# Attention pairs turned through two banks at once, a reciprocal of two columns, and packed score matmuls in a chunked recurrence core, in a three-layer fp32 kernel

## The reference

```python
def swa_sink_attention(q, k, v, sinks, slopes):      # 8 query heads of 64, window 128
    scores = jnp.einsum('bnqhgd,bnkhd->bnhgqk', qb, kw)
    logits = jnp.where(valid[None, :, None, None], scores + alibi, -jnp.inf)
    m = jnp.maximum(logits.max(axis=-1), sink)
    p = jnp.exp(logits - m[..., None])
    denom = p.sum(axis=-1) + jnp.exp(sink - m)
    o = jnp.einsum('bnhgqk,bnkhd->bnqhgd', p, vw) / jnp.moveaxis(denom, 4, 2)[..., None]

def dsa_attention(q, k, v, qi, ki, wi):              # 8 heads of 64, the best 128 keys of each query
    score = jnp.einsum('bqh,bqhs->bqs', wib, jax.nn.relu(jnp.einsum('bqhd,bsd->bqhs', qib, ki32)))
    _, idx = lax.top_k(jnp.where(visible[None], score, -jnp.inf), topk)
    ...
    p = jax.nn.softmax(logits, axis=-1)
    return jnp.einsum('bhqk,bqkhd->bqhd', p, v_sel)

def hgrn2_chunked(q, k, v, log_f):                   # 4 heads, keys and values of 128
        inter = jnp.einsum('bhtd,bhde->bhte', qc * jnp.exp(bc), S)
        decay = jnp.exp(jnp.where(causal[:, :, None], bc[:, :, :, None, :] - bc[:, :, None, :, :], -jnp.inf))
        A = jnp.einsum('bhtd,bhsd,bhtsd->bhts', qc, kc, decay)
        intra = jnp.einsum('bhts,bhse->bhte', A, vc)
        S = jnp.exp(b_last[:, :, 0, :])[..., None] * S + jnp.einsum('bhsd,bhse->bhde', kc * jnp.exp(b_last - bc), vc)
```

## Time and profile before

| | |
|---|---|
| time, median of three runs | 2794.81 us |
| the profiled execution | 2796.15 us |
| its span (first to last instruction) | 2794.4 us |
| PE, matmuls | 94% busy, 12478 of them |
| PE, weight loads (overlap matmuls) | 76% |
| DVE / ACT / POOL | 42% / 36% / 38% |
| mean share of full clock that PE was granted | 0.97 |

### The profile page before, as it was taken

How to read it: one execution, slowest core, us unless ns; L and a number is a source line. 1 busy time by engine, 2 the same in 40 slices (tenths; PEclk the granted TensorE clock), 3 DMA queues, 4 the chain that set the end, 5 groups by cost and what they waited for, 6 DMA issues and landing times.

```text
span 2794.4 us, 30147 instructions
## 1 busy us (share of the span) xinstructions
PE 2626.1 (94%) x12478; PEld 2136.2 (76%) x12478; DVE 1172.5 (42%) x1924; ACT 994.9 (36%) x1152; POOL 1074.0 (38%) x816
## 2 busy tenths in 40 slices
PE   6999999999999979888999999999888899999999
PEld 5887777878888777776687888888767668788887
DVE  5243343365523546668625111133666772521112
ACT  3423443343323444425424222235432542432221
POOL 4323333544545442213244544543221324454452
PEclk8999999999999989999999999999999999999999
DMA  4222212222323221111122323223111212232232
GB/s 148 63 76 76 76 61 76 91 92 94 102 91 98 91 68 46 35 57 61 31 92 92 103 91 106 91 91 91 46 36 42 65 40 91 91 101 95 92 104 76
DMA packets 206707, 221.05 MB, mean 79 GB/s; under 512 B 3713, under 2 KB 197467, under 8 KB 206443
## 3 DMA queue, kind: packets, MB, share of 16 engines
q1 hardware_dynamic: 206064, 218.97, 24.5%
q10 hardware_dynamic: 507, 0.15, 0.0%
HBM read 217.01 MB, written 2.10 MB: 78 GB/s over the span
## 4 chain that ended last, share of the span: by engine, by line
PE 79%; DVE 12%; ACT 7%; DMA 1%; issue 1%; DVEq 0%; SPq 0%; ACTq 0%
PE psum L442 70%; PE psum L567 2%; ACT wh L912 2%; PE psum L684 1%; DVE dec L1521 1%; PE psum L672 1%; DMA raw<-in_w_in 1%; PE psum L663 1%; DVE score L1844 1%; DVE ul L1706 1%; DVE top L1842 1%; DVE ul L1417 1%; ACT dec L1038 1%; DVE merged L1729 1%; DVE normed L1478 1%
## 5 line engine op out<-in xcount | busy, mean ns | idle before, releaser
L896 POOL TENSOR_TENSOR wl<-raw,wh 128x512 fp32r<-128x512 f32 x812 | 1073.8, 1356 | 1694.4 <-ACT wh L912 1694.4
L442 PE MATMUL psum<-uh,wh 128*128 128x512 f32 x2024 | 811.8, 401 | 17.8 <-DVE ul L1706 4.4
L442 PE MATMUL psum<-ul,wh 128*128 128x512 f32 x2024 | 797.9, 394 | 0.0
L442 PE MATMUL psum<-uh,wl 128*128 128x512 f32 x2024 | 797.0, 394 | 0.0
L912 ACT CAST wh<-raw 128x2048 fp32r<-128x2048 f32 (+1 forms) x206 | 387.0, 1879 | 313.5 <-DMA raw<-in_w_ffn_out 117.6
L442 PEld LDWEIGHTS psum<-uh,wh 128*128 128x128 f32 x2024 | 386.8, 191 | 110.0 <-issue 14.5
L442 PEld LDWEIGHTS psum<-uh,wl 128*128 128x128 f32 x2024 | 385.9, 191 | 82.8
L442 PEld LDWEIGHTS psum<-ul,wh 128*128 128x128 f32 x2024 | 386.9, 191 | 79.0 <-issue 1.9
L442 PE MATMUL psum<-fh,wh 128*128 128x512 f32 x528 | 205.4, 389 | 0.0
L442 PE MATMUL psum<-fl,wh 128*128 128x512 f32 x528 | 205.4, 389 | 0.0
L442 PE MATMUL psum<-fh,wl 128*128 128x512 f32 x528 | 205.4, 389 | 0.0
(11 more groups left out here) (314 smaller groups left out, 3343.7 us busy)
## 6 DMA issues: line engine op xcount, KB each, us to landing
raw<-in_w_in SPq DMA_DIRECT2D x78, 1024.0 KB, 5.2
raw<-in_w_ffn_in SPq DMA_DIRECT2D x44, 1024.0 KB, 5.1
raw<-in_w_up SPq DMA_DIRECT2D x22, 1024.0 KB, 5.1
raw<-in_w_ffn_out SPq DMA_DIRECT2D x16, 1024.0 KB, 5.1
raw<-in_w_down SPq DMA_DIRECT2D x8, 1024.0 KB, 5.0
raw<-in_w_out SPq DMA_DIRECT2D x8, 1024.0 KB, 5.1
raw<-in_w_ffn_out SPq DMA_DIRECT2D x8, 768.0 KB, 4.3
raw<-in_w_o SPq DMA_DIRECT2D x4, 1024.0 KB, 5.0
```

The lines of the kernel that those rows point to most:

```text
L442: ins = mm(dst, x, y, start=first and i == 0, stop=last and i == len(todo) - 1)
L896: ins = nc.gpsimd.tensor_tensor(wl[p % 3][:, w], raw[p % 3][:, w], wh[p % 3][:, w].bitcast(F32), ALU.subtract)
```

## The change

**Core.** A level's matmul computes only the columns that are used: the moving operand is the odd blocks of `dec` (64 columns for each head), so a level takes 128 columns of PSUM instead of 256. Levels 0 and 1, the diagonal (now issued first) share `X[1]`, levels 2 and 3 with 4 to 6 fill `X[2]` and `X[3]`; nothing is overwritten, and PE's wait in the middle is gone. Slots 2 and 3 of the side steps now both stand behind the last level. DVE copies the diagonal with one 128x256 copy, then seven levels of 128x128 out of the odd blocks. Where DVE's slot 2 stood inside the copies, it now stands behind them.

**Attention.** `turn_probs` turns both heads at once, head 0 into `X[0]` (the scores' own bank) and head 1 into `X[2]`; ACT copies both with one instruction; the scores of pair i + 2 come behind the side steps and that copy. PE therefore waits for `logit_done`, that DVE has read the scores of pair i + 1 or i + 2, ahead of the transposes. DVE takes the reciprocal of two columns and spreads it with a copy. One (window) or two (sparse) side steps move between the first and the second scores. In the sparse layers the last block's keys are scored before pair 0, and the selection has 16 and 11 rounds ahead of the two halves of `core_post` in place of 14 and 14.

```diff
-SIDE_POST_2 = (4, 4)
-SIDE_WINDOW = [8, 9, 9, 10]
-SIDE_SPARSE = [4] * NT
-SELECT_EARLY = 14
+SIDE_POST_2 = (4, 2)
+SIDE_WINDOW = (1, [7, 9, 9, 10])
+SIDE_SPARSE = (2, [4] * NT)
+SELECT_EARLY = (16, 11)
+LEVEL_ENDS = (1, 3, 6)
+        def odd_blocks(x, l):
+            w = P >> (l + 1)
+            return x.rearrange("p (g two w) -> p g two w", two=2, w=w)[:, :, 1, :]
+        def level_scores(l):
+            w = P >> (l + 1)
+            at = l + 2 if l < 4 else l + 4
+            return X[1 + at // 4][:, P * (at % 4):P * (at % 4 + 1)].rearrange("p (h g w) -> p h g w", h=2, w=w)
...
-                    for l in range(LEVELS + 1):
-                        if l < LEVELS:
-                            pe.wait_ge(S.lev_ready, t.up(S.lev_ready))
-                        if l == 6:
-                            take_on(side, core_steps(total, u, 2))
-                            pe.wait_ge(S.pairs_done, t.up(S.pairs_done))
+                    for i in range(2):
+                        h = 2 * hp + i
+                        ins = mm(X[1][:, i * P:(i + 1) * P], gk[:, h, tok], gq[:, h, tok], start=True, stop=True)
+                    for l in range(LEVELS):
+                        pe.wait_ge(S.lev_ready, t.up(S.lev_ready))
                         for i in range(2):
-                            h, c = 2 * hp + i, 2 * P * (l % 2) + i * P
-                            lhs, rhs = (dec[:, i, l, :], dec[:, i, l, :]) if l < LEVELS else (gk[:, h, tok], gq[:, h, tok])
-                            ins = mm(X[1 + l // 2 % 3][:, c:c + P], lhs, rhs, start=True, stop=True)
-                        if l % 2 == 1:
+                            ins = mm(level_scores(l)[:, i, :, :], dec[:, i, l, :], odd_blocks(dec[:, i, l, :], l),
+                                     start=True, stop=True)
+                        if l in LEVEL_ENDS:
                             ins.then_inc(S.att_done, 1)
+                    take_on(side, core_steps(total, u, 2))
                     take_on(side, core_steps(total, u, 3))
-                    pe.wait_ge(S.pairs_done, t.up(S.pairs_done, 3))
+                    pe.wait_ge(S.pairs_done, t.up(S.pairs_done))
...
-                def turn_probs(i, e):
+                def turn_probs(i):
                     b0, b1 = blocks(HEAD_PAIRS[i][0])
-                    if e or i > 0:
-                        pe.wait_ge(S.pt_read, t.up(S.pt_read))
-                    for b in range(b1 - b0):
-                        ins = nc.tensor.transpose(X[2][:, b * P:(b + 1) * P], prob[i % 2][:, e, b * P:(b + 1) * P], ident)
+                    for e in range(2):
+                        for b in range(b1 - b0):
+                            ins = nc.tensor.transpose(X[2 * e][:, b * P:(b + 1) * P],
+                                                      prob[i % 2][:, e, b * P:(b + 1) * P], ident)
                     ins.then_inc(S.pt_done, 1)
...
                 qk(0)
+                take_on(side, first_steps)
+                pe.wait_ge(S.logit_done, t.up(S.logit_done))
                 qk(1)
                 if indexed:
                     index(NT - 1)
                 for i, (m, p) in enumerate(HEAD_PAIRS):
+                    if i + 1 < len(HEAD_PAIRS):
+                        pe.wait_ge(S.logit_done, t.up(S.logit_done))
                     pe.wait_ge(S.prob_done, t.up(S.prob_done))
-                    turn_probs(i, 0)
+                    turn_probs(i)
                     if i > 0:
                         pv(i - 1)
                     take_on(side, share(side_steps[m], AH // 2, p))
-                    turn_probs(i, 1)
+                    pe.wait_ge(S.pt_read, t.up(S.pt_read))
                     if i + 2 < len(HEAD_PAIRS):
                         qk(i + 2)
...
-                    nc.scalar.copy(probT[:, e, 0:kk], X[2][:, 0:kk]).then_inc(S.pt_read, 1)
+                    turned = X4.rearrange("p (e b) t -> p e b t", b=2)[:, :, 0, 0:kk]
+                    nc.scalar.copy(probT[:, :, 0:kk], turned).then_inc(S.pt_read, 1)
...
-                    v.reciprocal(inverse[:].rearrange("p (e d) -> p e d", e=2), st[:, 4:6].unsqueeze(2).to_broadcast([P, 2, HD])).then_inc(S.inverted, 1)
+                    v.reciprocal(st[:, 0:2], st[:, 4:6]).then_inc(S.dve_chain, 1)
+                    dve.wait_ge(S.dve_chain, t.up(S.dve_chain))
+                    v.tensor_copy(inverse[:].rearrange("p (e d) -> p e d", e=2),
+                                  st[:, 0:2].unsqueeze(2).to_broadcast([P, 2, HD])).then_inc(S.inverted, 1)
```

More of the change, by code:

```diff
@@ L1113, in indexed, with attention @@
                 act.wait_ge(S.i_scored, t.up(S.i_scored))
-            def attention(blocks, sink, side, side_steps):
+            def attention(blocks, sink, side, first_steps, side_steps):
                 def exps(i):
@@ L1387, in _ @@
                 core_post(side, SIDE_POST_2)
-                attention(lambda m: (0, m + 1), False, side, SIDE_SPARSE)
+                attention(lambda m: (0, m + 1), False, side, *SIDE_SPARSE)
                 n.merged = 0
@@ L1616, in core_post @@
                     if selection:
-                        take_on(selection, SELECT_EARLY)
+                        take_on(selection, SELECT_EARLY[j])
                     next_pair()
@@ L1632, in core_post, with attention @@
                     take_on(side, side_steps[j])
-            def attention(blocks, sink, side, side_steps, selection=None):
+            def attention(blocks, sink, side, first_steps, side_steps, selection=None):
                 dst = sq if sink else aq
@@ L1682, in attention @@
                 front(0)
+                take_on(side, first_steps)
                 front(1)
+                if selection:
+                    score_keys(NT - 1)
                 for i, (m, p) in enumerate(HEAD_PAIRS):
@@ L1687, in attention @@
                     back(i)
-                    if selection and i == 0:
-                        score_keys(NT - 1)
                     if selection and i < SELECT_LATE[1]:
@@ L2108, in _ @@
                 core_post(V_HN + l, True, side, SIDE_POST_2, selection)
-                attention(lambda m: (0, m + 1), False, side, SIDE_SPARSE, selection)
+                attention(lambda m: (0, m + 1), False, side, *SIDE_SPARSE, selection)
                 finish(merge(late, last=True))
```

51 lines of the change are left out of this document (26 added, 25 removed).

## The result

The changed kernel takes 2809.26 us (median of four runs, 2807.68 to 2810.79) beside 2794.60 for the one before (four runs, 2788.82 to 2797.06): a ratio of 1.0055, 95% interval 1.0038 to 1.0073. It is 15 us slower where a forecast of 2793 us called it a draw. The profiled executions are 2807.68 and 2796.15 us, with spans of 2805.9 and 2794.4.

What follows compares the result with a forecast made beforehand. TensorE was taken to bound the kernel, busy nearly throughout, so time could come only from its idle and lost clock. Core -19.5, sparse +20.4, window -3.0 sum to -2.1; 2796.15 - 2.1 - 1.3 gives 2793 us, range 2779 to 2813.

Steps and rivals of the forecast that it cites:

- The stall ahead of level 6: Core: PE's 18.6 us wait for DVE to empty the bank of levels 0 and 1 goes, priced at 18.5.
- The price of a pass: Core: the weight load alone fills a pass of 0.11 or 0.12 us, so halving the moving columns gains nothing.
- rival C: Core: passes go by their moving columns, 0.05 us less each, 13 us in all, so 2780 us; chance 0.14.
- For cold stretches that the new waits may bring I give back 2.5: Core: 2.5 us of the gain given back for clock lost behind the new waits.
- the core's -19.5: Core, packed scores: 19.5 us less in all, with bounds of 0 and -28.
- The new wait of the sparse pairs: Sparse loop: PE can't transpose until DVE has read the scores, a new wait of 1.4 to 2.7 us in 14 pairs.
- The sum of the sparse loop, +10.2 a layer: Sparse attention: +8.7 for the pairs' periods, +2 for clock, -0.4 ahead of the loop; +20.4 in both layers.
- rival B: Sparse loop: two in three of 24 new waits are followed by half clock, 22 us more, 2815 us; chance 0.18.
- The time ahead of the loop: Sparse attention before pair 1 is turned: moved selection rounds and gate steps shorten PE's 7.01 us stall, -0.4 us.
- Window, -3.0: Window attention: new waits cost 14.7 us; stalls for ACT's second copy, idle and cold stretches go; 3.0 us less.
- rival D: Core: the gain is passed on to the next late arrival, half of 19.5 stays, 2803 us; chance 0.13.
- The chances: Whole kernel: 0.34 faster (under 2789.2 us), 0.32 slower (over 2800.4), 0.34 between.

Runs made afterwards that it cites:

- scores_first: The changed kernel with the scores of pair i+2 ahead of the side steps in all three attentions, read by DVE before its selection rounds and evictions: 2819.9 us, ratio 1.0107.

## Why the prediction was wrong

The forecast was a draw from two large terms that cancel, with 2793 as its time; the kernel became 15 us slower. The mechanisms were all there, in the places named; two large terms were mis-sized, both to the bad side, by 9 and 7 us.

- **The stall ahead of level 6**: right. 18.6 us went to 0, with 8.4 ahead of the outputs (six of 1.0 to 1.5 us, forecast 1 to 2). The first unit came to the point: the output starts 7.5 us behind the first level matmul (1071.00 to 1078.54), where the forecast had 7.6.
- **The price of a pass**: right. Narrow and wide passes take 0.116 and 0.12 us, so half the moving columns save almost nothing, and rival C is out: its 0.05 us a pass came out under 0.01. About 105 ns for a load of 128 columns is the prediction's own estimate, from the 187 to 192 and 137 ns of the earlier trace rows; these passes are 10 to 14% longer, and no run changes the load alone.
- **"For cold stretches that the new waits may bring I give back 2.5", and with it the core's -19.5**: this step failed. I priced the halved columns at nothing because they change no pass, and looked for lost clock only behind new waits. It lay behind the old ones: PE came back from the same waits for DVE's first level with matmuls of half the columns and stayed at half clock (0.50) for 6.8 to 10.2 us where it had 3.4 to 6.8. So the cold stretches that I booked as gained behind the stalls came back there, 17 us more at half clock in four places, worth 8.5. The term measures 10 (7 to 14) for 19.5. Why the clock returns later behind narrower matmuls stays open.
- **The new wait of the sparse pairs**: right in place, and its single waits are somewhat shorter than forecast (1.0 to 1.9 us in most pairs, two over 2, one of 0.75; forecast 1.4 to 2.7). Of the fifteen periods eleven came within 0.2 us of the forecast, in the first layer: pairs 2 and 3 5.7 and 7.1 for 5.7 and 7.1, pairs 10 to 13 7.7, 7.4, 7.6 and 7.9 for 7.7, 7.3, 7.5 and 7.9, the last two together 12.2 for 12.2.
- **The sum of the sparse loop, +10.2 a layer**: mis-sized; +13.6 measured. Pairs 1 to 15 took 106.1 us from the first transpose (1300.98) to the dense matmul at 1407.08, where the forecast had 101 and 2 for clock. Four periods make the difference: pair 1 took 8.1 for 6.3, pair 4 7.3 for 6.1, pair 9 8.4 for 7.0, all three at half clock for a part (0.50 to 0.55, below), and pair 8 7.5 for 6.8, with the copy of 1.0 us beside POOL. Read as clock, the first three cost 4.4 and not 2. That is more than I allowed on top of the periods, not more than before: in the whole stretch PE spent 20.5 us at half clock in both kernels. A piece of rival B came true: not two in three of the new waits, but the two longest, 2.57 and 2.13 us, were each followed by 3.4 us at half clock. The third stretch, in pair 1, stands behind a wait of 2.55 us for ACT's copy and one of 0.75 for the scores' reading. The time ahead of the loop, -0.4 forecast, is +0.1 (66.1 us to the turn of pair 1, 66.0 before).

Windows of the changed kernel inside pairs 1, 4 and 9:

```profile
1302.00:1306.00 4.00, 4.00 (x12) 2.92 (x12) 3.24 (x10) 2.17 (x2) 1.14 (x1) 0.50 0.00 0
1323.00:1326.00 3.00, 3.00 (x8) 2.31 (x9) 2.83 (x8) 0.59 (x1) 0.00 (x0) 0.52 0.01 5
1357.50:1361.00 3.50, 3.50 (x14) 2.60 (x11) 2.73 (x8) 0.80 (x1) 0.00 (x0) 0.55 0.00 0
```

- **Window, -3.0**: -2.7 in this profile, about -1 on the mean of the profiles, so that the near hit is in part luck. **Passing on (rival D)**: the parts add up, so no.
- **The chances**: 0.32 lay on slower. Both large terms left out clock that was then lost, so their errors added up instead of cancelling.

## What to carry to other kernels

A bank that two steps share made the engine that reads it a part of the writer's loop: in the window the transposes waited 14.6 us for the scores' reading, and 0.4 with both heads in a bank of their own. So before merging two transposes into two banks, look for one bank that holds both. Side work hid a wait only where it stood between the last write and the engine that has to answer: DVE's reading of the scores cost PE 56.9 us ahead of the transposes in the change and 0.7 in scores_first. But don't put it behind the engine that also evicts and casts, where PE then waited 3.4 to 8.4 us three times in each sparse loop. Where the weight load fills a pass, as by the estimate from the earlier trace rows in this core, fewer moving columns gain almost nothing (0.116 us a pass for 0.12); read the granted clock behind the waits before and after such a cut.

## What the runs showed of the hardware

- The kernel with the wider matmuls was the faster one: with five of seven levels at 128 columns instead of 64, and the same number of passes and the same waits, it has 0.9978 and not 1.0003. Behind the waits of the last two units of both cores, PE ran 10 to 17 us at half clock (0.50) in the three profiles with 128 columns in all levels, 14 with five wide levels, 20 and 27 with three, and 24 to 41 in the eleven with none.
- The core with the same packed code took from 196.7 to 202.1 us in the first of its layers, in the profiles of different kernels, and from 193.0 to 200.8 in the other, depending on which of its waits were followed by half clock. One profile is one draw; a few microseconds in such a stretch need timed runs.
- A DVE copy of 128x128 in SBUF takes 0.23 us alone. In ten of its 48 places in the changed kernel it stood beside a POOL subtraction, and nine of these took 1.0 to 1.4 us.
